# A pooling-mixer and SwiGLU trunk on one core: the first w_out group loaded from ScalarE's queue, two orders of sums changed, one matrix for the meta tokens

## What is computed

```python
h = concat([meta, x])                                  # 16 + 2048 rows
u = h @ w_in                                           # 1024 x 1024, four groups of 256 columns
pooled = trailing mean of u over 2, 4, 8, 16 rows      # one window per group
y = einsum('gc,gce->ge', pooled - u, w_group)          # 256 x 256 per group
m = (y * scale) @ w_out
h = layer_norm(ALPHA * h + m, ln_mix_g, ln_mix_b)
gate, up = split(h @ w_gu)                             # 2 x 2816 columns
h = layer_norm(ALPHA * h + (silu(gate) * up) @ w_down, ln_ffn_g, ln_ffn_b)
return h[16:]
```

## Time and profile before

| what | value |
|---|---|
| runs | 1665.40, 1661.54, 1656.80 us; median 1661.54 |
| the profiled execution | 1657.87 us |
| its span in the profile | 1656.1 us |
| TensorE matmul busy | 1639.9 us, 99% |
| TensorE weight loads | 1355.9 us, 82% |
| VectorE | 1050.9 us, 63% |
| ScalarE | 616.5 us, 37% |
| GpSimd | 649.1 us, 39% |
| granted TensorE clock, mean | 0.999 |
| DMA | 330.84 MB, 200 GB/s over the span |

### The profile page before, as it was taken

How to read it: one execution, slowest core, us unless ns; L and a number is a source line. 1 busy time by engine, 2 the same in 40 slices (tenths; PEclk the granted TensorE clock), 3 DMA queues, 4 the chain that set the end, 5 groups by cost and what they waited for, 6 DMA issues and landing times.

```text
span 1656.1 us, 19058 instructions
## 1 busy us (share of the span) xinstructions
PE 1639.9 (99%) x7318; PEld 1355.9 (82%) x7318; DVE 1050.9 (63%) x1085; ACT 616.5 (37%) x836; POOL 649.1 (39%) x439
## 2 busy tenths in 40 slices
PE   8999999999999999999999999999999999999998
PEld 7888888877888888888888888888888888888886
DVE  6779876987444444445756676776644434467866
ACT  5334465446333333333533333333333332322220
POOL 0440025015347666654456566666631000341002
PEclk9999999999999999999999999999999999999999
DMA  9674378444357566565656666666668543564542
GB/s 342 245 289 167 130 260 299 175 147 183 115 165 235 190 204 226 181 223 190 228 176 205 220 217 212 191 205 197 193 205 289 176 156 128 196 223 172 201 141 94
DMA packets 190954, 330.84 MB, mean 200 GB/s; under 512 B 8464, under 2 KB 132496, under 8 KB 181136
## 3 DMA queue, kind: packets, MB, share of 16 engines
q1 hardware_dynamic: 151168, 297.64, 52.4%
q10 hardware_dynamic: 37520, 23.60, 4.7%
q0 software_dynamic: 2176, 8.39, 1.3%
HBM read 227.36 MB, written 102.24 MB: 199 GB/s over the span
## 4 chain that ended last, share of the span: by engine, by line
PE 94%; DVE 2%; POOL 1%; DMA 1%; issue 1%; ACT 1%; SPq 0%; POOLq 0%; DVEq 0%; ACTq 0%
PE acc L1227 42%; PE acc L1256 19%; PE acc L1060 11%; PE turn L1227 7%; PE turn L1256 6%; PE acc L1094 5%; PE turn L1094 3%; DMA raw<-w_out 1%; PE turn L1048 1%; PE acc L1137 1%; DVE stats L1753 0%; DVE wf L1823 0%; DVE split L1777 0%; POOL rstd L889 0%; POOL wr L883 0%
## 5 line engine op out<-in xcount | busy, mean ns | idle before, releaser
L1227 PE MATMUL acc<-fa,wf 128*128 128x512 f32 x1584 | 366.6, 390 | 2.3 <-DVE acc L1942 1.7
L1227 PE MATMUL acc<-fb,wf 128*128 128x512 f32 x1584 | 363.4, 389 | 0.4 <-DVE acc L1942 0.4
L1227 PEld LDWEIGHTS acc<-fb,wf 128*128 128x128 f32 x1584 | 297.1, 188 | 63.0 <-issue 1.4
L1227 PEld LDWEIGHTS acc<-fa,wf 128*128 128x128 f32 x1584 | 295.8, 188 | 64.3 <-DVE wf L1823 3.0
L1256 PE MATMUL acc<-dw,da 128*128 128x512 f32 x1386 | 315.3, 389 | 0.0
L1256 PEld LDWEIGHTS acc<-dw,da 128*128 128x128 f32 x1386 | 260.1, 188 | 54.0
L1823 DVE TENSOR_TENSOR wf<-wt,wf 128x512 fp32r<-128x512 f32 x132 | 139.9, 1061 | 157.0 <-ACT wf L1428 156.6
L1823 DVE TENSOR_TENSOR wf<-wr,wf 128x512 fp32r<-128x512 f32 x176 | 177.7, 1014 | 51.4 <-ACT wf L1428 51.0
L883 POOL TENSOR_TENSOR wt<-wr,wt 128x512 f32<-128x512 f32 x88 | 136.1, 1546 | 169.4 <-DVE wf L1823 169.2
L1428 ACT CAST wf<-wr 128x512 fp32r<-128x512 f32 x176 | 108.6, 618 | 210.4 <-PE acc L1227 204.9
L1060 PE MATMUL acc<-mov,split 128*128 128x512 f32 x768 | 177.5, 391 | 0.0
(11 more groups left out here) (138 smaller groups left out, 1807.6 us busy)
## 6 DMA issues: line engine op xcount, KB each, us to landing
wr<-w_gu SPq DMA_DIRECT2D x44, 1024.0 KB, 5.2
dar<-af_dram SPq DMA_DIRECT2D x56, 704.0 KB, 4.4
af_dram<-g ACTq DMA_DIRECT2D x32, 512.0 KB, 5.8
raw<-w_in SPq DMA_DIRECT2D x15, 1024.0 KB, 7.6
fs<-hf_dram SPq DMA_DIRECT2D x14, 1024.0 KB, 5.6
dt_raw<-w_down SPq DMA_DIRECT2D x22, 512.0 KB, 6.0
wt_dram<-dt_t SPq DMA_DIRECT2D x22, 512.0 KB, 4.2
sa<-af_dram SPq DMA_DIRECT2D x22, 512.0 KB, 8.3
```

What stands on the lines that cost most here:

```text
L1227: mm = nc.tensor.matmul(dst, wf[:, slot, a, k, :], fa[half][i][:, v, :, k, :], start=i < 2 and k == 0 and n3 == 0, stop=k == KC - 1 and n3 ...
```

## The change

Four things change.

1. The four pieces of group 0 of `w_out` are issued from ScalarE's queue as the first thing that ScalarE does, and no longer from SyncE's between the loads of `scale` and of the second piece of `w_group`.
2. GpSimd makes a matrix `parts` of 64x16 (the sum of two slices of the identity) at the start, and `meta_features` uses it: one matmul for each half in place of two. The result is the same sum.
3. In VectorE's list, for the second half of the tokens: the adds of t = 5 come ahead of `form_lo(3)`, and of the adds of t = 6 the one of row tile 0 comes after two of the four `unit_lo` in place of after all four.
4. In GpSimd's list, `rstd_of(3)` comes after T1 to T4 of unit 2 in place of ahead of them.

```diff
@@ -153,6 +153,8 @@
         rows = [at(f"rows{n}", V0 + n * 4 * KB, [P, D]) for n in range(2)]
 
         ident = sb("ident", [P, P])
+
+        parts = sb("parts", [2 * LO_AT, N_META])
         scale_sb = sb("scale_sb", [P, KT])
         mix_g_sb = sb("mix_g_sb", [P, KT])
         mix_b_sb = sb("mix_b_sb", [P, KT])
@@ -475,9 +477,9 @@
             def load_wout(grp):
                 if grp >= 2:
                     sp.wait_ge(wout_lo_ready, wout_before(grp - 1))
-                for n, (e, cols) in enumerate(WOUT_PIECES[grp]):
-                    landed = wout0_landed[n] if grp == 0 else wout_landed[grp % 2][e]
-                    sp.dma_start(raw[:, grp % 2, e * D:(e + 1) * D][:, cols], w_out[grp, :, e, cols]).then_inc(landed, 16)
+                for e, cols in WOUT_PIECES[grp]:
+                    sp.dma_start(raw[:, grp % 2, e * D:(e + 1) * D][:, cols], w_out[grp, :, e, cols]
+                                 ).then_inc(wout_landed[grp % 2][e], 16)
 
             def load_x(b, i):
                 if b:
@@ -677,7 +679,6 @@
 
             load_group(0)
             sp.dma_start(scale_sb[:], scale).then_inc(scale_landed, 16)
-            load_wout(0)
             load_group(1)
             load_wout(1)
             sp.dma_start(meta_sb[:], meta_t).then_inc(meta_landed, 16)
@@ -979,6 +980,9 @@
             pool.wait_ge(ident_zero, 1)
             nc.gpsimd.affine_select(out=ident[:], in_=ident[:], compare_op=ALU.not_equal, fill=1.0, base=0,
                                     pattern=[[-1, P]], channel_multiplier=1).then_inc(ident_ready, 1)
+            pool.wait_ge(ident_ready, 1)
+            nc.gpsimd.tensor_tensor(parts[:], ident[0:2 * LO_AT, 0:N_META], ident[0:2 * LO_AT, LO_AT:LO_AT + N_META],
+                                    ALU.add).then_inc(ident_ready, 1)
             nc.gpsimd.memset(minus_half[:], -0.5).then_inc(half_ready, 1)
             pool.wait_ge(half_ready, 1)
             nc.gpsimd.memset(zeros[:], 0.0).then_inc(zeros_ready, 1)
@@ -994,7 +998,6 @@
             unit_t4(0)
             unit_t123(1)
             unit_t4(1)
-            rstd_of(3)
             for n in range(UNITS):
                 half, jj = n // HALF_UNITS, n // 2
                 if n % 2 == 0 and jj - 1 >= JF:
@@ -1007,6 +1010,8 @@
                     up22_times_gate(jj)
                 if n + 2 < UNITS:
                     unit_t4(n + 2)
+                if n == 0:
+                    rstd_of(3)
                 for e in range(2):
                     if n in TF_STEP[e]:
                         tform(e, TF_STEP[e][n])
@@ -1141,14 +1146,12 @@
             def meta_features(i):
                 pe.wait_ge(meta_rows_staged, i + 1)
                 if i == 0:
-                    pe.wait_ge(ident_ready, 1)
+                    pe.wait_ge(ident_ready, 2)
                 else:
                     pe.wait_ge(meta_u_taken, i)
                 for m in range(2):
-                    for v in range(2):
-                        mm = nc.tensor.matmul(acc[:, 5, m * H:(m + 1) * H], meta_rows[:, m * P:(m + 1) * P],
-                                              ident[0:2 * LO_AT, v * LO_AT:v * LO_AT + N_META],
-                                              start=v == 0, stop=v == 1)
+                    mm = nc.tensor.matmul(acc[:, 5, m * H:(m + 1) * H], meta_rows[:, m * P:(m + 1) * P], parts[:],
+                                          start=True, stop=True)
                 mm.then_inc(meta_u_done, 1)
 
             def mixer_block(b):
@@ -1357,6 +1360,10 @@
                 nc.scalar.copy(fold_st[:, grp, 0, :].rearrange("p (a n) -> p a n", a=2),
                                pair(2 * grp % 3)).then_inc(fold_a_staged, 1)
 
+
+            for n, (e, cols) in enumerate(WOUT_PIECES[0]):
+                nc.scalar.dma_start(raw[:, 0, e * D:(e + 1) * D][:, cols], w_out[0, :, e, cols]
+                                    ).then_inc(wout0_landed[n], 16)
             group_hi(0)
             act.wait_ge(scale_landed, 16)
             wout_hi(0)
@@ -1729,8 +1736,8 @@
                 e, cols = {1: (0, 0), 3: (1, 1), 4: (0, 1), 5: (1, 1), 6: (1, 0)}[t]
                 return zm[e][:, m, cols * TOK:(cols + 1) * TOK]
 
-            def add_rows(h, t):
-                for m in range(TT):
+            def add_rows(h, t, tiles=range(TT)):
+                for m in tiles:
                     rows_ = row_half(h, t, m)
                     if t in (1, 3):
                         dve.wait_ge(z_landed[t // 3][m], 16 * (h + 1))
@@ -1867,8 +1874,13 @@
                         d_lo(h, t + 1)
                     if h and t == NP - 1:
                         form_lo(4)
-                        for q in range(4):
-                            unit_lo(0, q)
+                        unit_lo(0, 0)
+                        unit_lo(0, 1)
+                        add_rows(h, t, (0,))
+                        unit_lo(0, 2)
+                        unit_lo(0, 3)
+                        add_rows(h, t, range(1, TT))
+                        form_lo(5)
                     if t in (2, 5) or h == 0 and t == 6:
                         rows_stats(h, t - 1)
                     if t == 5:
@@ -1877,12 +1889,12 @@
                     if h == 0 and t in (0, 1, 2, 4):
                         x_lo(2, (0, 1, 2, 4).index(t))
                     if h:
-                        for q in ((), (0,), (1,), (2,), (), (3,), ())[t]:
+                        for q in ((), (0,), (1,), (2,), (), (), ())[t]:
                             form_lo(q)
-                    if t in (1, 3, 4, 5, 6):
+                    if t in (1, 3, 4, 5) or h == 0 and t == 6:
                         add_rows(h, t)
-                    if h and t == NP - 1:
-                        form_lo(5)
+                    if h and t == 5:
+                        form_lo(3)
 
             for h in range(2):
                 mixer_block(2 * h)
```

## The result

| kernel | median, us | lowest to highest | runs |
|---|---|---|---|
| before, beside it | 1658.72 | 1656.02 to 1665.40 | 6 |
| with the change | 1666.38 | 1664.47 to 1668.18 | 6 |

The ratio is 1.0045, with a 95% interval of 1.0029 to 1.0060. The change makes the kernel slower, by 7.5 us at that ratio. The median lies above the forecast of 1660.6 us and above the upper end of its range, 1664.8 us. The profiled execution took 1668.18 us, its span is 1666.4 us, 10.3 us more than the 1656.1 before.

The account below looks back on a forecast made before the run. TensorE, busy 1639.9 of 1656.1 us, was taken as the bound. Parts 2, 1, 3 and 4 summed as -2.0 - 0.4 + 0.2 + 1.3 = -0.9 us, median 1661.54 to 1660.6 us, range 1655.0 to 1664.8.

Parts of the forecast that it names:

- the saving of part 2: Meta-token matmuls on TensorE: two in place of four save 0.50 us a visit, 2.0 us at four visits.
- the price of a wait: TensorE's waits: the forecast counted each wait at its own length only.
- Anything that is saved stays saved unless a later wait eats it: TensorE, full between 7.4 us of waits: the four parts can only move these waits or shorten TensorE's work.
- None of them reaches 8.3 us, as all waits together are 7.4.: Whole kernel: no rival reaches the 8.3 us (0.5%) that a measurement can tell from no change.
- Part 1, -0.4 us, bounds -2.0 and +2.0.: Start loads: fourth piece near even at +0.4 us, and the 0.8 us wait at the first w_in chunk closes by about 0.7.
- the 413 GB/s: Start loads: if two queues lift the DMA rate to this, the fourth piece comes up to 1 us earlier.
- rival C: Start: pieces share the DMA engines, fourth piece 2.1 us late; sum +2.4 us, median 1663.9; chance 0.2.
- over 1.5 us late: Start: fourth-piece lateness from which the slower case decides, since part 2's 2.0 us must be outweighed.
- Part 3, +0.2 us.: VectorE's sums: the 1.64 us wait at t = 6 returns as a wait for ScalarE's copy; bounds -2.1 and +0.6.
- Part 4, +1.3 us, bounds 0 and +1.8.: Unit 1: rstd behind T4 starts norm 0.8 us later, plus a GpSimd turn; +0.8 to +2.0 before ScalarE's slack.
- 1.2 us at most: Unit 1: T1 falls onto VectorE's wf ahead of the statistics for rstd, costing one more GpSimd turn.

Follow-up runs that it names:

- e2: Kernel before with part 2 alone (one matrix for the meta tokens): 1659.43 us, ratio 1.0014.
- e5: Kernel before with part 2 and a second buffer for GpSimd's pair sums, so the second pair need not await the first's store: 1655.47 us, ratio 0.9984.
- e13: Kernel before with only a second buffer for GpSimd's pair sums added: 1656.72 us, ratio 0.9990.
- e14: Kernel before with part 1 (w_out's first group on ScalarE's queue) and the second pair-sum buffer: 1660.11 us, ratio 1.0010.
- e15: e14 plus eleven idle matmuls where TensorE would wait before the fold: 1658.21 us, ratio 0.9997.
- e3: Kernel before with part 3 alone (order of VectorE's sums): 1656.70 us, ratio 1.0004.
- e12: Whole change plus second pair-sum buffer, e8's T-form order, e7's start loads, and block 2's norms behind ScalarE's copy, their stores behind unit 2's weight loads: 1650.32 us, ratio 0.9952.
- e4: Kernel before with part 4 alone (rstd of the last block behind unit 2's T forms): 1661.12 us, ratio 1.0030.
- e8: Kernel before with GpSimd doing T1 to T3 of unit 2, then rstd of block 3, then T4: 1655.49 us, ratio 0.9980.
- e7: Kernel before with SyncE issuing the four w_out pieces first, ScalarE only w_group's first piece and scale: 1656.42 us, ratio 1.0004.

## Why the prediction was wrong

The forecast was a gain of 0.9 us, and the kernel lost 7.5. Four steps failed: the saving of part 2 was taken as kept, the price of a wait left the clock out, part 1 had the wrong sign, and part 4 was too small.

**"Anything that is saved stays saved unless a later wait eats it", part 2's "it stays saved".** The size was right (4.2 to 2.5 us of busy matmuls). The step fails on GpSimd's store chain: e2 alone is 2.4 us slower, and e5, which differs from e2 by the second buffer and its semaphores alone, is 1.9 us faster than the kernel before beside it (1657.33). The list of waits could not show the chain, as it was 0 in the one profile that I read, but the timeline did: GpSimd stood 7.93 us for its own store, and the three runs spread from 1656.80 to 1665.40. The spread was read as noise of the measurement; e13 suggests that a good part of it was this wait.

**"None of them reaches 8.3 us, as all waits together are 7.4."** This bounds what can be gained, not what can be lost. New waits are not bounded by the old ones: 13.5 us, and 5.9 of clock.

**The price of a wait.** Every term of the sum was the wait's own length. Nothing in the earlier trace rows shows a low clock, since waits of 1.6 to 1.7 us passed without one there. With the change they are longer, or two close together, and each of the four places has one. This is the largest step missing, and e14 against e15 measures it at 1.9 us for the start.

**Part 1, -0.4 us, bounds -2.0 and +2.0.** Wrong in sign, and out of bounds once the clock counts: +3.4 by e14 against e13, of which 1.5 without the clock. The rate rose far less with two queues than to the 413 GB/s that the value leaned on: in the windows of 2 us from 2 to 8 us the DMA engines moved 247, 290 and 253 GB/s with the change, against 193, 264 and 250 before. That is rival C's mechanism, with the fourth piece 1.3 us late in place of 2.1. The point from which C was to decide ("over 1.5 us late") was wrong too. The Trainium skill, "DMA: Bandwidth & Descriptors", section "Issuing engines are not separate DMA queues", has another issuing engine save only the time of issuing; the trace agrees in the main (253 against 250 GB/s once both kernels had all four pieces issued). I took a value between that and a rate for which no row spoke.

**Part 3, +0.2 us.** Right in which waits go and come: the 1.64 us at L1094 went and ScalarE's copy became the new wait, of 1.05 us (1 to 2 forecast). Net it is -0.8 us in the waits, near the middle of the bounds. The reason given was not right. T3, and with it the copy, was to come 0.3 to 1.1 us later. In e3 T3's cast starts at 375.58 us against 376.25 before, and the copy at 384.54 against 385.20: neither is late, TensorE is early. GpSimd's `rstd` took 1.03 us there, beside the adds, and not 3.00 beside a form. e12 shows that moving the norms in front of the copy is enough to end the wait.

**Part 4, +1.3 us, bounds 0 and +1.8.** Right in sign and place, too small. The wait was to be 2.5 to 3.5 us and is 4.06. From T4's start to `norm` it took 3.69 us where 3.6 were summed. But the form before T4 also came 1.2 us later than the shift of TensorE explains (413.48 against 404.44 + 0.68 + 7.19 = 412.31). The text had this turn of GpSimd's as "1.2 us at most" beside the 0.8, a sum of 2.0 that the bound of 1.8 and the value of 1.3 both cut short for a slack that isn't there. The low clock adds 1.3 us here (48 matmuls in 12.46 us against 11.16), and 2.7 in e4.

**The 1.4 us at 89 us** were no part of any case. The wait also shows in the profiles of e3 (1.17) and e8 (1.51), so it is no property of the whole change, and no wait over 0.3 us stands there in the other fourteen profiles. In those three GpSimd starts its work ahead of `d`, and `d` and `mov` take 2.19 to 2.29 us each; in the fourteen it starts after both have started, and they take 1.22 or 1.23. So the wait goes with the moment at which GpSimd's data lands. No run changed that moment alone.

The balance of the two profiles: waits +6.1, low clock +5.9 (the rest of the busy time; 4.7 of it read directly), meta tokens -1.7, together the 10.3 us of the spans.

The chances in the prediction add up to 1.03 and not to 1.

**Still open.** Why the same store takes 8 or 13 us: the DMA engines move 354 GB/s from 247 to 249 us and then only 160 and 250 in the next two windows of 2 us, where before they moved 350, 236 and 393 from 244 to 250. No changed line runs then, so the change can only have shifted the time at which these transfers meet. Also open is why a wait of 3.13 us in e2 had no low clock and one of 3.12 us in e7 did.

## What to carry to other kernels

Where TensorE is busy for 99% of the time, price a new wait of a few us at its length and a low-clock stretch behind it (1.3 to 2.7 us here, though a wait of 3.13 us in e2 had none), and close it with idle matmuls if it can't be removed (tried here at the start of the kernel only). Before moving an instruction ahead of another on an in-order engine, ask what the moved one waits for: T1 to T3 ahead of `rstd` saved 1.5 us of a wait, T4 ahead of it added 3.9. And when runs of one kernel fall into two groups, look for a chain with thin margin, here one buffer behind its own store, before trusting that a saving will be kept.

## What the hardware showed that was not expected

- Waits as short as 1.39 us (at 89 us) were followed by the level of 1.2 GHz; waits of 1.64 and 1.74 us in the kernel before were not. 192 matmuls took 45.44 us behind that wait in the changed kernel, and 43.81 in e3, where a wait of 1.17 us left the clock up.
- The same store of 1 MB by GpSimd kept GpSimd waiting for 7.9 to 8.4 us in five profiles and for 12.4 to 12.8 in four, and for nothing between.
- The same two instructions of VectorE (`d` and `mov`, 128x1024) took 1.22 us each when GpSimd's work started after them, and 2.2 to 2.3 us when it started ahead of them (before, and with the change, at 84 to 89 us).
- Eleven matmuls on idle data made a kernel 1.9 us faster (e15 against e14).
